# Two-layer decoder trunk on one core: where half banks of the output projections are issued, and how x is turned ahead of the second mixer

## The reference

```python
for i in range(DEPTH):                       # 2 layers
    h = _rmsnorm(x, norm)
    x = x + mixer(h)                         # i = 0: fox, i = 1: dilated; both end in o @ w_out
    x = x + square(relu(_rmsnorm(x, mlp_norm[i]) @ mlp_w1[i])) @ mlp_w2[i]
# fox: q, k, v = h @ w_in, q and k RMS-normed per head, causal softmax with a decay, 16 heads of 64
# dilated: 3 groups (window, dilation) = (128,1), (512,4), (2048,16), each its own q, k, v;
#          q, k RMS-normed and partly rotated; outputs merged by softmax of their log-sum-exps
```

## Time and profile before

| | |
|---|---|
| time, median of 3 runs | 1581.89 us (1580.29 to 1582.23) |
| the profiled execution | 1582.23 us, its span 1580.1 us |
| mean granted TensorE clock | 0.995 |
| PE busy | 1535.6 us (97% of the span) |
| DVE, ACT, POOL busy | 934.2, 706.4, 381.6 us |
| chain that ended last | PE 80%, DVE 8%, POOL 5% |

### The profile page before, as it was taken

One profiled execution on the slowest core, in us unless ns is written; L12 is line 12 of the kernel. 1 busy time (PEld: TensorE's weight loads), 2 busy tenths in 40 slices (PEclk: granted clock), 3 DMA queues, 4 the chain that ended last, 5 costly groups with the idle time before them and its releaser, 6 DMA issues.

```text
span 1580.1 us, 24697 instructions
## 1 busy us (share of the span) xinstructions
PE 1535.6 (97%) x9276; PEld 1235.9 (78%) x9284; DVE 934.2 (59%) x1642; ACT 706.4 (45%) x1188; POOL 381.6 (24%) x513
## 2 busy tenths in 40 slices
PE   7999999999999999799999999999999999999998
PEld 6777766888888887678878877888877888888886
DVE  5456644557474848754646577655654556565658
ACT  6433344354454545534434344443453454535353
POOL 2301100021101611162427354333711110101010
PEclk9999999999999999899999999999999999999999
DMA  6221110466575654333222412222223476575753
GB/s 177 81 64 44 54 41 15 147 142 178 133 179 137 153 155 94 120 86 88 68 80 82 136 55 66 81 81 73 77 95 112 131 158 186 121 198 109 198 118 80
DMA packets 111600, 173.57 MB, mean 110 GB/s; under 512 B 12688, under 2 KB 45456, under 8 KB 111504
## 3 DMA queue, kind: packets, MB, share of 16 engines
q1 hardware_dynamic: 91904, 134.51, 27.5%
q0 software_dynamic: 17408, 33.56, 13.1%
q10 hardware_dynamic: 2192, 4.20, 0.7%
HBM read 165.89 MB, written 6.36 MB: 109 GB/s over the span
## 4 chain that ended last, share of the span: by engine, by line
PE 80%; DVE 8%; POOL 5%; issue 3%; ACT 2%; DMA 1%; SPq 1%; DVEq 0%; POOLq 0%; ACTq 0%
PE ps L594 53%; PE ps L896 15%; PE ps L657 3%; PE ps L711 3%; PE ps L685 2%; PE ps L723 2%; POOL qrs L1747 1%; DVE w_l L1557 1%; PE ps L625 1%; DMA raw<-in_mlp_w 1%; ACT p_sb L1046 1%; DVE e_all L1603 1%; DVE qn L1332 1%; POOL rt L1756 1%; DVE x_sb L1619 1%
## 5 line engine op out<-in xcount | busy, mean ns | idle before, releaser
L594 PE MATMUL ps<-w_h,act_h 128*128 128x512 f32 x768 | 311.7, 406 | 9.3 <-DVE w_l L1278 3.5
L594 PE MATMUL ps<-w_h,act_l 128*128 128x512 f32 x768 | 303.7, 395 | 0.0
L594 PE MATMUL ps<-w_l,act_h 128*128 128x512 f32 x768 | 303.2, 395 | 0.0
L1278 DVE SCALAR_TENSOR_TENSOR w_l<-w_raw,gain_t,w_h 128x512 fp32r<-128x512 f32 x188 | 143.5, 805 | 112.7 <-ACT w_h L972 112.6
L594 PE MATMUL ps<-act_h,w_h 128*128 128x512 f32 x512 | 200.1, 391 | 1.0 <-DVE w_l L1528 1.0
L594 PE MATMUL ps<-act_l,w_h 128*128 128x512 f32 x512 | 199.5, 390 | 0.0
L594 PE MATMUL ps<-act_h,w_l 128*128 128x512 f32 x512 | 199.5, 390 | 0.0
L594 PEld LDWEIGHTS ps<-w_h,act_h 128*128 128x128 f32 x768 | 152.9, 199 | 39.4 <-issue 11.9
L1747 POOL TENSOR_TENSOR qrs<-qss,m_half 128x8 f32<-128x8 f32 x64 | 105.3, 1646 | 320.9 <-DVE qss L1317 320.3
L1046 ACT ACTIVATE p_sb<-ps,negmax 128x128 f32<-128x128 f32 (+4 forms) x256 | 88.1, 407 | 206.2 <-DVE negmax L1371 111.6
L896 PE MATMUL ps<-w_h,op_h 128*128 128x512 f32 x448 | 175.8, 392 | 0.1
(11 more groups left out here) (215 smaller groups left out, 2437.5 us busy)
## 6 DMA issues: line engine op xcount, KB each, us to landing
w_raw<-in_dil_w_in SPq DMA_DIRECT2D x72, 512.0 KB, 3.7
raw<-in_mlp_w SPq DMA_DIRECT2D x64, 512.0 KB, 4.6
raw<-in_mlp_w POOLq DMA_DIRECT2D x48, 512.0 KB, 5.7
w_raw<-in_mlp_w SPq DMA_DIRECT2D x32, 512.0 KB, 4.8
w_raw<-in_fox_w_in SPq DMA_DIRECT2D x22, 512.0 KB, 3.7
p_sb<-in_mlp_w SPq DMA_DIRECT2D x16, 512.0 KB, 5.6
pT_sb<-in_mlp_w SPq DMA_DIRECT2D x16, 512.0 KB, 6.3
w_raw<-in_mlp_w POOLq DMA_DIRECT2D x16, 512.0 KB, 6.5
```

The costliest lines, as they stand in the source:

```text
L594: return mm(ps_out, lhs[i], rhs[j], start=(k == 0 and term == 0), stop=(k == KT - 1 and term == 2))
L1278: last = v.scalar_tensor_tensor(w_l[u % WR][:, j, :], raw(u)[:, j, :], gain_t[:, norm, k:k + 1], f(w_h[u % WR][:, j, :]), ALU.mult, ALU.su ...
```

## The change

Five edits. (a) Sets 0 and 2 (`ALONE`) use a ring of three PSUM banks (`RING`); `turn_qk` moves to slice 4 (6 for the first) and DVE sums the squares ahead of the unit of weights. (b) The first halves of three banks of each output projection (12 times 3 matmuls) are issued at the ticks of `FILL_TICKS`, between `turn_probs` and `values`; banks 0 to 3 lie in four PSUM banks, and `out_projection` begins with the first half of bank 3. (c) Transposes of x behind output banks move (`TURNED_BEHIND`). (d) In the last chunk of each MLP 16 DVE operations of the sums are done between the hidden banks (`earlier_sums`), ACT copies the product A11_B11 from PSUM, and 22 operations are left behind the products; POOL makes one small operation more (`xneg`). (e) For set 2 x is transposed by column tiles: 16 transposes between the two halves of A22_T4, 16 behind slice 2 of bank 0 of set 2, whose second half comes after the first half of bank 1. ACT and DVE now read PSUM with a stride of 128 numbers and write `act_h`, `act_l` without a gap.

```diff
-PREP_AFTER_MLP = [(0, 1), (1, 1), (2, 0), (3, 0), (0, 0), (1, 0), (2, 1), (3, 1)]
+RING = [0, 1, 2, 0, 1, 2, 0, 1, 2, 1, 0, 1]
+ALONE = [0, 2]
+FILL_TICKS = {1: [7, 9, 11, 13, 15, 17, 19, 21, 23, 24, 25, 26], 7: [5, 7, 9, 10, 11, 12, 13, 14, 15, 16, 17, 18]}
+TURNED_BEHIND = {4: [(0, 0), (0, 1)], 5: [(0, 2), (0, 3)], 6: [(1, 0), (1, 1)], 7: [(1, 2)]}
...
+        def bank_of(B):
+            for s, third in zip(ALONE, (ps_s[0], ps_p[0])):
+                if 0 <= B - set_bank0(s) < NB_SET:
+                    return (ps_proj[0], ps_proj[1], third)[RING[B - set_bank0(s)]]
+            for first in (BANK_FOX_OUT, BANK_DIL_OUT):
+                if 0 <= B - first < NT:
+                    return (ps_proj[0], ps_proj[1], ps_q, ps_s[0])[B - first]
+            return ps_proj[B % 2]
...
+        def prep_by_column(n, half, t):
+            k = 4 * half + t
+            return [ap.rearrange("p (m t) -> p m t", t=NT) for ap in (act_h[:, k, :], act_l[:, k, :])]
...
+                if n == 3:                                          # PE, prepare
+                    x_ready(pe, 2, 2 * half + 1, half)
+                    if half:
+                        pe.wait_ge(actl_done, prep_no(n, t, 0) + 1)
+                    for i in range(NT):
+                        last = nc.tensor.transpose(bank[:, i * P:(i + 1) * P], x_sb[:, i, pc % 8 * P:(pc % 8 + 1) * P], ident[:, :])
...
                         if 2 <= a <= nt + 1:
                             turn_probs(attend, t0 + a - 2)
+                        if proj is None:
+                            out_terms(attend, a)
                         if 3 <= a <= nt + 2:
                             values(attend, t0 + a - 3)
...
+                    if proj == 2:
+                        half = 3 * KT // 2
+                        terms = [*range(half), *range(2 * half, 3 * half), *range(half, 2 * half), *range(3 * half, len(terms))]
...
-                        if attend is None and k == 1 and term == 0 and 2 <= b <= QK_SET + 1:
+                        if attend is None and k == (6 if b == 2 else 4) and term == 0 and 2 <= b <= QK_SET + 1:
                             turn_qk(s, b - 2)
...
-                half = 3 * KT // 2                                  # PE, out_projection
-                prepared(prep, 0, 1)
-                terms(1, 0, 8)
+                half = 3 * KH
+                terms(3, 0, half // 2)
...
                 prepare(prep, 1, 0)
-                terms(1, 8, half)
                 prepare(prep, 1, 1)
+                terms(3, half // 2, half)
                 for b in range(8):
                     if b < NT:
                         prepared(prep, 1, b)
-                    terms(b, half if b < 2 else 0, 3 * KT)
+                    terms(b, half if b < NT else 0, 3 * KT)
...
+                    if final:                                       # ACT, chunk
+                        act.wait_ge(sums_added, layer + 1)
+                        for tau in range(2):
+                            act.wait_ge(proj_full, mlp_unit(layer, i, 8 + tau) + 1)
+                            nc.scalar.copy(e_sum[0][:, tau, :], mlp_ps[0][tau][:, :]).then_inc(e11_copied, 1)
...
-                split_low(B + 4)                                    # DVE, bank_event
+                if attend is not None or b >= QK_SET:
+                    split_low(B + 4)
...
-                if attend is None:
+                if attend is None and b < QK_SET:
+                    split_low(B + 4)
                     norm_qk(s, b)
...
-                def finish(q, tau, last):                           # DVE, mlp
+                def earlier_sums(step, tau):                        # behind hidden bank b: step b // 2, tau b % 2
+                    if step == 0:
+                        to_x(0, 1, tau, e11)
+                        link(v.tensor_tensor(e22, e22, e11, ALU.add))
+                    elif step == 1:
+                        to_x(0, 0, tau, e1)
+                        link(v.tensor_tensor(e33, e33, e22, ALU.add))
+                    elif step == 2:
+                        to_x(1, 0, tau, e1)
+                        link(to_x(0, 0, tau, e22, minus=True))
+                    else:
+                        to_x(1, 1, tau, e33)
+                        last = to_x(1, 0, tau, e33, minus=True)
+                def last_products(q, tau, ps_in):                   # A11_B11: 1 operation, S1_T1: 2
...
+                    if q == S2_T2:
+                        link(v.tensor_tensor(e22, e11, ps_in, ALU.add))
+                        return to_x(0, 0, tau, e22, minus=True)
+                    if q == S3_T3:
+                        link(v.tensor_tensor(e33, e22, ps_in, ALU.add))
+                        to_x(1, 1, tau, e33)
+                        return to_x(1, 0, tau, e33, minus=True)
...
-                    last = g.tensor_tensor(xaux[:, norm, :], xrs[:, norm, :], xrs[:, norm, :], ALU.mult)
+                    link(g.tensor_tensor(xaux[:, norm, :], xrs[:, norm, :], xrs[:, norm, :], ALU.mult))
+                    last = g.tensor_scalar(xneg[:, norm // 2, :], xaux[:, norm, :], -1.0, None, ALU.mult)
```

More of the change, by code:

```diff
@@ L310, in trunk @@
         xaux = sb("xaux", [P, 5, NT])
+        xneg = sb("xneg", [P, 2, NT])
         qss = sb("qss", [P, 2, HS])
@@ L469, in wait_bank_free @@
         def wait_bank_free(pe, B):
-            if B >= 2:
-                kind, n = bank_kind(B - 2)
-                pe.wait_ge({"qk": qn_done, "v": v_done, "x": x_added}[kind], n + 1)
+            for before in range(B - 1, max(B - 5, -1), -1):
+                if bank_of(before) is bank_of(B):
+                    kind, n = bank_kind(before)
+                    pe.wait_ge({"qk": qn_done, "v": v_done, "x": x_added}[kind], n + 1)
+                    return
         block = ctx.enter_context(nc.Block())
@@ L905, in chunk @@
                         if final and layer == 0 and q == A22_T4:
-                            prepare(3, 0, 0)
-                            prepare(3, 0, 1)
+                            for t in range(4):
+                                prepare(3, 0, t)
                         seventh(i, q, 1)
-                        if final and layer == 0 and q in (S3_T3, S4_B22):
-                            for t, half in PREP_AFTER_MLP[2 * (q - S3_T3):2 * (q - S3_T3) + 2]:
-                                prepare(3, half, t)
                     if not final:
@@ L1203, in chunk @@
                                 split_high(BANK_DIL + u)
-                        if final and layer == 0 and q >= S3_T3:
-                            for t, half in PREP_AFTER_MLP[2 * (q - S3_T3):2 * (q - S3_T3) + 2]:
-                                prepare(3, half, t)
                             if q == A22_T4:
+                                for t in range(4):
+                                    prepare(3, 0, t)
                                 keep(0)
@@ L1681, in mlp @@
                 if layer == 0:
-                    prepare(3, 1, 2)
-                    prepare(3, 1, 3)
+                    for t in range(4):
+                        prepare(3, 1, t)
             t_g_rows = sq[0:NH, :]
```

130 lines of the change are left out of this document (70 added, 60 removed).

## The result

The changed kernel takes 1557.24 us (median of 4 runs, 1556.66 to 1558.50), the kernel before 1581.95 in the runs beside it. The ratio is 0.985, with a 95% interval of 0.983 to 0.986: 24.7 us less, where 20.6 were forecast. The profiled execution has a span of 1554.9 us against 1580.1.

The account below looks back on a forecast made before the run. PE, busy 97% of the span, was taken as the bound, with DVE bounding the passage from MLP 0 to set 2. Seven terms sum to 20.6 us off 1582.2, 1561.6, adjusted to the runs' median: 1561.3 us, range 1554.5 to 1571.5.

Parts of the forecast that it names:

- more than forecast: Rival: the 2.0 us wait leaves the clock up and fills hide all; 1556 us, chance 0.12.
- (1): Set 0, third bank: PE's 1.57 us wait before bank 2 goes and nothing takes its place; 1.6 us less.
- (6): Starts of both MLPs: POOL's extra operation delays clearing `e_sum`, 0.13 to 0.27 us each; 0.5 us more.
- (2): Attention of set 1: fills cover waits, except three odd ticks whose loop lengthens by 0.67 us; 3.8 us less.
- (3): MLP 0 into set 2: DVE reaches the weights 7.3 us earlier, PE waits 2.0 us; 9.5 us less.
- The rival of 1563 us: Rival: strided PSUM reads are slow, DVE's subtractions and ACT's copies as before; 1.7 us less gain, chance 0.12.
- (4): Set 2, three banks: waits for rotated q and k shrink, 1.0 us of wait left; 2.2 us less.
- (5): Attention of set 7: nine fills delay `values` 3.2 us, but 22 more matmuls are done by then; 1.8 us less.
- (7): The end: DVE is free when the last matmul ends, leaving one addition; 2.2 us less.
- The slower one: Rival: in each MLP's last chunk the moved sums delay weight splits and PE waits; 1588 us, chance 0.03.
- Fills stretch the loops: Rival: each fill lengthens its loop fully, so (2) and (5) give nothing; 1567 us, chance 0.09.
- Bound by the loads: Rival: in the turn into set 2 two loads come back late; 6.2 us less gain, 1567.5 us, chance 0.14.

Follow-up runs that it names:

- The kernel with the nine late matmuls: Changed kernel with 9 of 36 output-projection matmuls in set 7's attention moved behind its values, before the last head's transposes: 1555.99 us, 0.984 of before.
- both parts undone: Changed kernel with the moved sums of the hidden banks (d) and the column tiles (e) undone together: 1569.57 us, 0.992 of before.

## Why the prediction was right, and where it was not

The forecast of 20.6 us was 4 short of the 24.7 measured, inside its range; the order and the mechanisms of the large terms held. The measured 1557.24 us is nearer to the rival "more than forecast" (1556) than to the forecast (1561.3), and half of that rival came true: the clock stayed up in the profiled execution, but the fills did not hide all. The sum came out as near as it did partly by luck, since (1) and (6) promised 1.6 us too much and the other terms too little. By its own steps:

**(1), forecast 1.6, measured 0.5 against the first profile of before and -0.4 against the second or against the kernel without the ring.** The step that failed is "so nothing takes the wait's place". I followed PE's wait for qn and did not go on along ACT's queue: the evacuation of turned q stands in it ahead of the copies of x for bank 3, so that transposes of q four microseconds later held those back. Transposes of q two slices into the bank, and not six, bring the gain. Moreover the 1.57 us were one execution's; in the other it was 0.72.

**(2), forecast 3.8, measured 4.8 for the whole part,** of which 4.1 by undoing the fills. The term was right, and so were its three ticks that lengthen the loop: between the scores of 256 and of 512 columns it is 4.38 us for 3.92, 0.46 for each where 0.67 was put in. The other 0.7 (1.0 before the longer wait in (6) is taken off) lies behind the attention, to which I gave nothing.

**(3), forecast 9.5, measured 10.7.** By the old times, with the 4.64 us gained ahead added, DVE came to the weights at 634.5 (635.0 forecast), PE waited 1.6 us for the additions (2.0), and bank 1 was done at 659.4 (660.9 with the 0.7 for the clock). Undoing the sums cost 5.8, their 5.8 us of DVE in full; undoing the tiles 3.3. What failed is the clock: I wrote that the length of the new wait makes the lower clock likely again, and took 0.7 off. In the profile after, neither that wait of 1.58 us nor the next of 2.60 lowered it. In the executions in which it fell behind the second wait the passage took 59.03 to 59.29 us for 68.64, so that the gain is 9.4 to 9.6: with the lower clock that it assumed, the term was right. The second wait itself was not in the sum: PE comes to bank 0 2.6 us ahead of the low part of turned x, which hangs on the late loads that stood in my sum.

The cost that no row showed, reading PSUM with a stride, was settled as taken. Durations of the two lines in the kernel after, in ns, least, median and most:

```profile
L1025 ACT CAST act_h<-ps x8: 562/593/618, 638.4 to 645.9; 128x512 fp32r<-128x512 f32 x8
```

```profile
L1329 DVE TENSOR_TENSOR act_l<-ps,act_h x8: 681/682/692, 640.5 to 646.8; 128x512 fp32r<-128x512 f32 x8
```

0.59 and 0.68 us against the 0.57 and 0.69 of the sum. The same two operations read PSUM in runs in set 0 of the same trace, with medians of 586 and 688 ns; the old copy with a strided write took up to 1128 ns. The Trainium skill ("Advanced Engine Details and Errata", section Memory Cachelines) asks that every two consecutive elements in PSUM lie together for best throughput. By that the new read, which goes to another line at each element, would be slow. The measurement decides: at a step of 512 bytes in PSUM nothing was lost, on ACT or on DVE. The rival of 1563 us is out.

**(4), forecast 2.2, measured 3.8.** No wait is left where I kept 1.0. With the old order of banks 0 and 1 the ring brings these 3.8 us (61.87 to 58.04). Beside (e) it is worth more: without it that kernel is 8.6 us slower up to the end of set 2, some of it by the clock, because (e) makes two banks too few. I had seen that the banks end 2.8 us apart, and used it only to lower the term, not to ask what (e) would cost without (a).

**(5), forecast 1.8, measured 3.6;** 0.9 of that is the fall of the clock at 1201 us in the first profile of before, which its second profile does not have; the longer wait in (6) is already taken off. The step by which the point behind the nine fills "comes 7.1 - 3.9 = 3.2 us later" overstates: beside the kernel with the fills undone the last scores come 1.7 us later (89.8 for 88.1 from the mark in set 6), and what follows is 4.8 us shorter. The wait did grow as I wrote (3.1 us, 3.5 forecast), but not through the additional fills: it is 3.1 without them too. Three matmuls of the last fill now stand ahead of `values`, and six instead of eight in front of the transposes, so PE has 1.1 us less to do behind the last values. That the clock is low behind this wait "before and after" did not hold: before, it fell in one profile of two, and after in neither of two.

**(6), forecast a loss of 0.5, measured 1.0:** the two waits rose from 1.0 to 2.0 us in total. The mechanism stands, since moving the clearing removes both; what was too small is the size, 0.13 to 0.27 us each for 0.3 and 0.7 measured. The clearing starts 0.46 us behind the start of the operation before it for 0.13 in both MLPs, so the extra operation costs 0.33. The other 0.35 in MLP 1 lie behind the clearing and stay open.

**(7), forecast 2.2, measured 2.35;** the last DVE operation starts 0.43 us behind the last matmul's start, one operation of 0.75 us.

**The rivals.** The slower one falls with the rows of DVE: 28.97 us busy in 44, with PE's time up to the products of the last chunk unchanged (244.79 and 244.80). "Fills stretch the loops" falls with the undone fills. "Bound by the loads" was no rival but the next bound: with these loads out of the way bank 2 starts 3.2 us sooner still.

**The clock.** The same kernel, where it fell or not, gives its price. From A11_B11 of the last chunk to bank 2 of set 2 the changed kernel takes 57.90 us with the clock up. The kernels with the early transposes of q, the early clearing and no additional fills are the same there; in their profiled executions the clock fell behind the wait of 2.6 to 2.8 us, and they take 59.29, 59.03 and 59.15: one fall of some 3.5 us costs 1.1 to 1.4 us. The kernel with the nine late matmuls has a wait of 2.78 us there, no fall, and 58.10. Between the pairs of executions with both parts undone the difference is 3.6 us. For the whole result it matters less: of the 24 executions of before that ran beside these kernels the two at 0.998 have spans of 1578.3 and 1578.5 us, those at 0.995 of 1579.5 to 1580.7, and the changed kernel's at 1.000 have 1554.8 to 1555.8. At the highest clock of each the difference is still 23 us. The kernel before was never at 1.000, so a part of these 23 us may still be the clock's. What decides in one execution whether the clock falls stays open.

## What to carry to other kernels

When a wait of the first engine is taken away by issuing an operation later, follow what the operation releases through the queue of the engine that drains it: the next need may stand right behind. Parts of a change should be undone one at a time even when all went well: one (the ring in set 0) was a small loss inside a gain, and another (the ring in set 2) is worth more beside its neighbour than alone. Undone one at a time, the four parts cost 8.3, 9.1, 3.9 and 9.5 us between the spans, 30.8 with the falls of the clock in them, for a change that gains 25.2: the prices of parts that share a path do not add. When a bound has been removed, the loads whose buffers it released are the next place to look; here two free buffers of the phase that had just ended brought 3.2 us.

## What was not expected of the hardware

- Reading PSUM at a step of 512 bytes cost nothing measurable: 593 ns on ACT and 682 ns on DVE for 128x512, where the same operations reading in runs take 586 and 688. With a step of 16 bytes in SBUF a subtraction takes 1.0 us (two in 2.04); DVE has that step in what it reads (`act_h`) and in what it writes, and no run separates the two.
- The granted clock fell to 0.50 at waits of 1.74 to 7.17 us, but not each time. It stayed at 1.00 behind 3.08 us in the profile of the changed kernel and behind 3.24 in that of the undone column tiles; behind 1.95 us it fell in one profile of the kernel before (there 1.94) and not in the other. The falls last some 3.5 or some 7 us.
- The first bank takes 18.07 to 19.18 us from the start in different executions, with the time at which PE's matmuls go from 0.43 to 0.23 us apart. So a gain of 1 us in a start-up is read from a later mark, not from the span.
